# Gathers for a mixture of 16384 experts on one Trainium2 core: the v gather issued 24 slots behind the u gather instead of 20

## What is computed

```python
def peer(h, w_q, sub_keys, u, v):
    q = (h @ w_q).reshape(B, T, PEER_HEADS, 2, PEER_QDIM // 2)
    s = jnp.einsum('bthpd,hpnd->bthpn', q, sub_keys)
    s1, i1 = lax.top_k(s[..., 0, :], PEER_TOPK)
    s2, i2 = lax.top_k(s[..., 1, :], PEER_TOPK)
    ...
    top_s, pos = lax.top_k(cand_s, PEER_TOPK)
    idx = jnp.take_along_axis(cand_i, pos, axis=-1)
    gate = jax.nn.softmax(top_s, axis=-1)
    ...
        act = jax.nn.gelu(jnp.einsum('td,ted->te', h_i, u[i_i]), approximate=False)
        return jnp.einsum('te,ted->td', (g_i * act).astype(h.dtype), v[i_i])
```

## Time and profile before

| | before |
|---|---|
| median of 3 runs | 3141.65 us (3134.77 to 3144.39) |
| span of the profiled execution | 3138.9 us |
| PE busy | 2537.8 us (81%) |
| DVE busy | 1695.8 us (54%) |
| POOL (GpSimd) busy | 1658.0 us (53%) |
| ACT busy | 602.9 us (19%) |
| moved by DMA | 960.99 MB, mean 306 GB/s |
| gathers of u and of v | 768 + 768, 512 KB each, 805.40 MB |

### The profile page before, as it was taken

How to read it: one execution, slowest core, us unless ns; L and a number is a source line. 1 busy time by engine, 2 the same in 40 slices (tenths; PEclk the granted TensorE clock), 3 DMA queues, 4 the chain that set the end, 5 groups by cost and what they waited for, 6 DMA issues and landing times.

```text
span 3138.9 us, 24534 instructions
## 1 busy us (share of the span) xinstructions
PE 2537.8 (81%) x7734; PEld 1231.7 (39%) x7734; DVE 1695.8 (54%) x4121; ACT 602.9 (19%) x1412; POOL 1658.0 (53%) x1540
## 2 busy tenths in 40 slices
PE   6998768888888898778887777777968888777777
PEld 3445643334454454223332322223654445222222
DVE  1224684544685676555545565642476557655552
ACT  1011112112231111111212122221202212211221
POOL 0000135554556656767665676771024665777775
PEclk9997889999989999999999999998977999999999
DMA  6462468998878899999999899994267899999998
GB/s 205 142 207 74 146 229 320 339 346 315 283 279 312 317 343 354 379 387 397 395 392 377 314 389 364 366 380 161 68 243 248 290 357 370 378 366 370 374 380 290
DMA packets 339774, 960.99 MB, mean 306 GB/s; under 512 B 27952, under 2 KB 112064, under 8 KB 339264
## 3 DMA queue, kind: packets, MB, share of 16 engines
q0 software_dynamic: 221184, 805.40, 68.7%
q1 hardware_dynamic: 114448, 146.53, 13.7%
q10 hardware_dynamic: 4016, 7.49, 0.7%
HBM read 958.27 MB, written 1.05 MB: 306 GB/s over the span
## 4 chain that ended last, share of the span: by engine, by line
PE 48%; DMA 16%; POOL 15%; DVE 9%; issue 7%; ACT 3%; ACTq 0%; SPq 0%; DVEq 0%; POOLq 0%
PE ps L681 21%; DMA v_rows<-in_peer_v,idx 14%; POOL v_rows L390 8%; PE ps L489 8%; POOL u_rows L390 8%; PE ps L424 5%; PE ps L654 4%; PE ps L620 3%; DVE u_rows L1293 2%; PE ps L414 2%; ACT diag L878 1%; PE ps L539 1%; PE ps L451 1%; PE ps L560 1%; PE ps L538 1%
## 5 line engine op out<-in xcount | busy, mean ns | idle before, releaser
L681 PE MATMUL ps<-v_rows,diag 128*128 128x512 f32 x3072 | 1503.2, 628 | 441.2 <-DMA v_rows<-in_peer_v,idx 296.7
L1293 DVE CUSTOM_DVE_ANT_0 u_rows<-u_rows,h 128x1024 f32<-128x1024 f32 x768 | 925.8, 1224 | 618.3 <-DMA u_rows<-in_peer_u,idx 614.9
L390 POOL DMA_INDIRECT u_rows<-in_peer_u,idx x768 | 816.4, 1063 | 819.0 <-DVE idx L1250 541.4
L390 POOL DMA_INDIRECT v_rows<-in_peer_v,idx x768 | 841.3, 1095 | 647.4 <-PE ps L681 510.9
L681 PEld LDWEIGHTS ps<-v_rows,diag 128*128 128x128 f32 x3072 | 561.4, 196 | 1287.0 <-issue 674.1
L878 ACT ACTIVATE diag<-table,act_w 128x128 f32<-128x128 f32 x768 | 279.3, 394 | 810.0 <-PE ps L681 737.5
L489 PE MATMUL ps<-wring,arena 128*128 128x512 f32 x576 | 256.6, 601 | 1.9 <-DVE arena L967 1.9
L654 PE MATMUL ps<-arena,wring 128*128 128x256 f32 (+1 forms) x1024 | 189.7, 343 | 7.0 <-DMA wring<-in_peer_w_q 4.9
L424 PE MATMUL ps<-wring,silu_c 128*2 128x256 f32 x768 | 177.5, 386 | 10.1 <-DMA wring<-in_mod_w 10.1
L654 PEld LDWEIGHTS ps<-arena,wring 128*128 128x128 f32 x1024 | 167.4, 204 | 36.4 <-issue 15.3
L489 PEld LDWEIGHTS ps<-wring,arena 128*128 128x128 f32 x576 | 110.9, 194 | 139.2 <-issue 135.3
(11 more groups left out here) (153 smaller groups left out, 1614.7 us busy)
## 6 DMA issues: line engine op xcount, KB each, us to landing
wring<-in_mod_w SPq DMA_DIRECT2D x48, 1024.0 KB, 8.4
wring<-in_peer_w_q SPq DMA_DIRECT2D x32, 1024.0 KB, 9.8
wring<-in_ab_w_in SPq DMA_DIRECT2D x28, 1024.0 KB, 5.2
wring<-in_swa_w_in SPq DMA_DIRECT2D x14, 1024.0 KB, 9.2
u_rows<-in_peer_u,idx POOLq DMA_INDIRECT x768, 6.3
v_rows<-in_peer_v,idx POOLq DMA_INDIRECT x768, 6.2
wring<-in_ab_w_out SPq DMA_DIRECT2D x8, 1024.0 KB, 8.1
wring<-in_swa_w_out SPq DMA_DIRECT2D x8, 1024.0 KB, 5.7
```

The source lines that it names most:

```text
L390: nc.gpsimd.indirect_dma_start(out=ring[:, j % nring, :], out_offset=None, in_=table, in_offset=bass.IndirectOffsetOnAxis(ap=IDX[:, g % NR ...
L681: mm = nc.tensor.matmul(PS[:, 6 + e, :], diag[:, j % NV, :], VB[:, j % NV, e * 512:(e + 1) * 512], start=s % S1 == 0, stop=s % S1 == S1 - ...
L1293: nc.vector.tensor_tensor_reduce(UB[:, j % NU, :], UB[:, j % NU, :], H2[:, g // 8 % 3, :], 1.0, 0.0, ALU.mult, ALU.add, av_[:, 0, g % 2, j ...
```

## The change

A new constant `PLAG` is 24 (20 + 8 - 4). GpSimd alone uses it, in place of `LAG`, for the distance between the u gather and the v gather that follows it, and for the length of its loop. PE, ACT and DVE keep 20, and so do the rings, their sizes and all waits' conditions.

```diff
@@ -45,6 +45,7 @@
 NV = 4
 NR = 4
 LAG = TOPK + 4
+PLAG = LAG + NU - NV
 
 
 T_ID = 0
@@ -394,14 +395,14 @@
 
             for T0, T1_ in WINDOWS:
                 l = TILE[T0][0]
-                for slot in range(S1 * T0, S1 * T1_ + LAG):
+                for slot in range(S1 * T0, S1 * T1_ + PLAG):
                     if slot < S1 * T1_:
                         if slot % TOPK == 0:
                             pool.wait_ge(routed, slot // TOPK + 1)
                         if slot >= NU:
                             pool.wait_ge(u_dot, slot - NU + 1)
                         gather(a[f"peer_u{l}"], slot // TOPK, slot % TOPK, UB, NU, u_in)
-                    s = slot - LAG
+                    s = slot - PLAG
                     if s >= S1 * T0:
                         if s >= NV:
                             pool.wait_ge(v_used, s - NV + 1)
```

## The result

| | before | changed |
|---|---|---|
| median on the same chip | 3139.63 us (4 runs, 3134.77 to 3144.39) | 3235.97 us (4 runs, 3233.73 to 3248.51) |
| ratio, 95% interval | 1 | 1.0303, 1.0273 to 1.0333 |
| span of the profiled execution | 3138.9 us | 3246.3 us |
| mean granted clock of TensorE | 0.945 | 0.934 |

What follows compares the result with a forecast made beforehand. Bound taken stage by stage: GpSimd with gathers alone, PE leading where the second pass's work runs beside. Terms -7.0 + 14 + 12 + 2.4 - 8 = +13.4 us on 3141.65 gave 3155 us, range 3130 to 3182.

Steps and rivals of the forecast that it cites:

- A v gather was issued behind the u gather of s + 20 ... now behind that of s + 24.: GpSimd's queue: a v gather of s now needs the dot product of s + 16, before that of s + 12.
- Output projection: a loss of 14 us: Six output projection steps inside the windows: each v gather goes out 2.3 us later, 14 us lost in all.
- group ends: 12 us: Six group ends in the top-k search: v gathers wait for a later dot product, 2.0 us each, 12 us lost.
- First steps of the first window: a loss of 2.4 us.: Start of the first window: v gather at 486.2 in place of 483.77 while PE idles for it, 2.4 us lost.
- Stretches with gathers alone: nothing.: Where only gathers run: u, v order stays, DVE moves 4 slots ahead, new condition is met early; no change.
- The fourth rival: Meetings of gathers and dot products shift: 11 us on top of the forecast or off it; chance 0.09, 0.05 up.
- The end of each window: a gain of 7.0 us.: Both window ends: four slots each move u gathers to earlier idle time of GpSimd, 3.5 us gained per window.
- The third rival: Transfers bound the mixed stretches and window ends give nothing: +20.4, 3162 us; chance 0.08.
- Two waits of DVE for u that hold up PE: a gain of 8 us.: Before second-pass attention and retention's group norm: u four slots ahead shortens PE's idle time, 5 and 3 us gained.
- The bound in stretches with gathers alone: From 2750 to 3050 us GpSimd was taken as full, 300.4 of 300 us in gathers and the gaps between them.

Runs made afterwards that it cites:

- sum20: The kernel before, with DVE's dot product replaced by a sum over the u row alone (one SBUF input for two): 3141.7 us, ratio 0.9894.

## Why the prediction was wrong

- **"A v gather was issued behind the u gather of s + 20 ... now behind that of s + 24."** Right, and so was the condition under which it costs. What failed is how the late events were priced.
- **"Output projection: a loss of 14 us", "group ends: 12 us".** This is the step that failed. I read how late one v gather is in the trace of before, 2.3 us, and multiplied by six. That number is the first round: PE's idle time before that v went from 0.25 us to 3.00. The late v makes PE's next step late, this DVE's step, this the next dot product, and a lateness grows until the circle itself sets the pace: 4.03 us a slot for 3.59 from 128 to 160, 14 us in 32 slots by itself. In slots 128 to 224 the loss was 36.0 us and not 12, in 512 to 608 22.1 and not 11. I had written that "the delay isn't made good by the next step" and did not ask whether the next step adds its own. The group ends could not be told apart from the rest.
- **"First steps of the first window: a loss of 2.4 us."** The first round again was right. The v gather that went out at 483.77 went out 4.4 us later, behind a u gather that waited for DVE:

```profile
486.15 1.68 POOL L391 DMA_INDIRECT u_rows<-in_peer_u,idx  x1 [7.28 <-DVE act_w L1294]
...
488.13 1.98 POOL L391 DMA_INDIRECT v_rows<-in_peer_v,idx  x1 [0.31 <-issue]
...
493.55 2.93 PE L682 MATMUL ps<-v_rows,diag 128*128 128x512 f32 x3 [3.69 <-DMA v_rows<-in_peer_v,idx]
```

  2.4 us of these 4.4 were foreseen. 1.2 more come from the dot product that it waited for, over at 485.88 and not at 484.66, and 0.7 from the u gather, 1.68 us beside the next dot product and not 0.94. Up to slot 64 the loss was 17.7 us, 9.9 of it up to slot 24 and 7.8 from there to 64. The projections had no term at all: I had looked for places where PE idled for v in the trace of before, and in them it did not.
- **"Stretches with gathers alone: nothing."** Hardly a wait for DVE appeared there (2.2 us), as forecast. But a pair of gathers took longer. The stretch from 2850 to 3150 us, for the earlier trace rows:

```profile
L391 POOL DMA_INDIRECT v_rows<-in_peer_v,idx x104 | 121.3, 1167 | 32.2 <-issue 19.8 <-PE ps L682 12.3
L391 POOL DMA_INDIRECT u_rows<-in_peer_u,idx x104 | 113.8, 1095 | 33.6 <-issue 31.4 <-DVE act_w L1294 2.2
```

  104 pairs for 107. The fourth rival had this, longer gathers, at 11 us and a chance of 0.05. Gathers took 19.1 us more in slots 224 to 480 and some 8 in 608 to 736. What I had not priced at all are GpSimd's waits for dot products in slots 224 to 480, 50.2 us, of which the fewer waits for PE made up 30. All of it is gone in the pair with one input; how the rest divides between the two is not settled.
- **"The end of each window: a gain of 7.0 us."** Right: 2.7 us from slot 480 to 511 and 4.8 from 736 to 767, 7.5 together. The third rival, which had the bytes as the bound and no gain here, falls.
- **"Two waits of DVE for u that hold up PE: a gain of 8 us."** Right in place. Slots 64 to 128, with the first of the two, gained 6.2 us, and PE's idle time of 5.33 us before the first bias multiplication is gone: the table is loaded while PE has other slots' matmuls. At the second, the group norm, PE's idle time of 4.60 us before the matmuls of slot 136 fell to 0.59; from the start of the matmuls of slot 133 to that of 139 it is 19.6 us for 22.6, the 3 us of the forecast.
- **The bound in stretches with gathers alone.** I named GpSimd. `sum20` took 205 us off its gathers, and slots 608 to 736 took 362.1 us for 357.3, on a chip on which before is 1% slower: not faster. GpSimd is idle for 119 of 361 us there, and the DMA engines are busy for 0.97 of the time at 371 GB/s (0.99 and 376 before). So shorter gathers give nothing there, and the transfers hold as well; as bytes they are what the third rival had as the bound, though its consequence, no gain at the ends, did not come. The Trainium skill (SBUF — State Buffer, "A bandwidth-pool intuition that's wrong") puts HBM's rate for one core at about 358 GB/s. By that the stretch could not have run at the 373 GB/s of the earlier trace rows, nor `sum20` at 371: the measurement decides. Whether the rate or the number of gathers in flight is the limit, no run separates.
- **The range.** Its upper end added up each term's bound, and each bound was one round of the circle. Most of the unknown lay in what a round does to the next.

## What to carry to other kernels

Before a transfer is moved in a queue that works in order, follow what it will wait for through all engines until the path comes back to its start, and divide the length of that circle by the slots that it spans: 20.34 us over five slots is 4.07 us a slot, and 32 slots that had run at 3.59 ran at 4.03. Pricing the first late event from the old trace, and multiplying, gives the first round alone. The distance of a gather and that of its consumers are one quantity with the ring size: moved together (24 on all engines) they were free; moved apart, two slots up were free too, but four up cost 3%, and so did two down.

## What the runs showed of the hardware

- **A gather's issue and DVE's operands.** Beside an operation of DVE with two inputs from SBUF a gather takes GpSimd up to 1.99 us, and beside one of the same length with one input mostly 0.94: the means of 1063 and 1095 ns fell to 948 and 944. The Trainium skill (SBUF — State Buffer, "SBUF: two separate sides") has GpSimd locked out of a shared port by DVE's operations with two SBUF inputs. The runs agree, with 115 and 151 ns a gather as the mean price. Where a gather is released by a dot product it starts beside the next one: in slots 64 to 224 of the changed kernel the 46 u gathers released so took 1421 ns on average, the other 114 took 1049.
- **PE is slower after it has waited.** PE's four matmuls of one slot take 1.98 us and took 3.60 at 1003.80, after PE had idled 3.00 us. The busy time in the changed kernel from 1003 to 1008 us and from 1008 to 1014 us (columns as in the earlier trace rows):

```profile
1003.00:1008.00 5.00, 4.20 (x6) 1.82 (x7) 0.00 (x0) 0.40 (x1) 3.78 (x5) 0.66 0.96 343
1008.00:1014.00 6.00, 6.00 (x15) 2.66 (x14) 0.00 (x0) 0.00 (x0) 1.83 (x2) 1.00 1.00 380
```

  The granted clock was 1.00 from 1000 to 1003 us and 0.66 in these 5 us, after 3.00 us of idle time, so part of them was at 1.2 GHz; it was 1.00, 2.4 GHz, once PE had work again. Over the whole kernel the same matmuls of line 682 took 36.1 us more, and PE's idle time before them grew by 71.0 (441.2 to 512.2): together 107.1 of the 107.4 us. No term of the forecast had the 36.1. How much of it made the kernel longer isn't shown: where PE waits for v rows anyway, slower matmuls cost nothing, and in `sum20` the same matmuls took 1523.2 us, 20 more than before, without a loss.
